# Forgetting attention: the per-head sums of squares of q and k in four reduced-precision passes over a high and a low half

## The reference, cut to what matters

```python
def fox_mixer(h, w_in, b_f, q_gain, k_gain, w_out):
    proj = h @ w_in
    q, k, v, g, f_logit = jnp.split(proj, [...], axis=-1)
    log_f = jax.nn.log_sigmoid(f_logit + b_f)
    qh = rms_norm(to_heads(q, FOX_HEADS), q_gain)   # y = x * rsqrt(mean(x*x over the 64 of a head) + EPS) * gain
    kh = rms_norm(to_heads(k, FOX_HEADS), k_gain)
    vh = to_heads(v, FOX_HEADS)
    o = fox_attention(qh, kh, vh, cumsum of log_f)  # causal softmax(q.k/8 + c[t] - c[s]) @ v
    return (o * jax.nn.silu(g)) @ w_out
```

## Time and profile before

| | |
|---|---|
| three runs, median | 1498.22 us |
| profiled execution, own time | 1497.39 us |
| its span (first to last instruction) | 1495.6 us |
| PE busy | 95% of the span |
| DVE busy | 64% |
| ACT busy | 47% |
| chain that ended last | PE 76%, DVE 13%, ACT 8% |

### The profile page before, as it was taken

One profiled execution on the slowest core, in us unless ns is written; L12 is line 12 of the kernel. 1 busy time (PEld: TensorE's weight loads), 2 busy tenths in 40 slices (PEclk: granted clock), 3 DMA queues, 4 the chain that ended last, 5 costly groups with the idle time before them and its releaser, 6 DMA issues.

```text
span 1495.6 us, 18290 instructions
## 1 busy us (share of the span) xinstructions
PE 1414.9 (95%) x7056; PEld 1190.4 (80%) x7056; DVE 955.8 (64%) x1333; ACT 703.5 (47%) x932; POOL 75.6 (5%) x82
## 2 busy tenths in 40 slices
PE   4899999999999999999979999999999999996996
PEld 3788887888888888888868889787878888885875
DVE  6898886444554444444469776546888778886474
ACT  4677767332342223222246444435456666565251
POOL 3000000000110000000020000020100000000211
PEclk9999999999999999999988999999999999997997
DMA  5111011322222232222311211322312111111211
GB/s 196 57 57 57 1 57 57 113 85 89 108 85 102 96 112 85 97 99 85 110 63 54 84 56 60 124 85 85 116 56 82 56 56 56 56 60 67 85 57 56
DMA packets 19242, 118.22 MB, mean 79 GB/s; under 512 B 2401, under 2 KB 3681, under 8 KB 5617
## 3 DMA queue, kind: packets, MB, share of 16 engines
q1 hardware_dynamic: 18896, 116.38, 21.8%
q0 software_dynamic: 288, 1.05, 0.2%
HBM read 115.32 MB, written 2.10 MB: 79 GB/s over the span
## 4 chain that ended last, share of the span: by engine, by line
PE 76%; DVE 13%; ACT 8%; issue 2%; DMA 0%; DVEq 0%; ACTq 0%
PE ps L508 23%; PE ps L510 23%; PE ps L509 23%; DVE wlo L1637 2%; PE ps L975 1%; PE ps L698 1%; PE ps L944 1%; DVE att L1894 1%; DVE acc L384 1%; ACT att L1217 1%; PE ps L579 1%; DVE atlo L1898 1%; PE ps L962 1%; ACT att L1215 1%; ACT att L1213 1%
## 5 line engine op out<-in xcount | busy, mean ns | idle before, releaser
L508 PE MATMUL ps<-uhi,whi 128*128 128x512 f32 x1104 | 442.5, 401 | 8.4 <-DVE ulo L1698 3.0
L510 PE MATMUL ps<-uhi,wlo 128*128 128x512 f32 x1104 | 433.1, 392 | 0.0
L509 PE MATMUL ps<-ulo,whi 128*128 128x512 f32 x1104 | 432.9, 392 | 0.0
L1637 DVE TENSOR_TENSOR wlo<-wraw,whi 128x2048 fp32r<-128x2048 f32 x105 | 243.5, 2321 | 103.1 <-ACT whi L1088 101.6
L1088 ACT ACTIVATE whi<-wraw 128x2048 fp32r<-128x2048 f32 x105 | 200.3, 1908 | 178.8 <-PE ps L510 178.4
L508 PEld LDWEIGHTS ps<-uhi,whi 128*128 128x128 f32 x1104 | 209.3, 190 | 56.6 <-issue 9.6
L510 PEld LDWEIGHTS ps<-uhi,wlo 128*128 128x128 f32 x1104 | 209.3, 190 | 45.4
L509 PEld LDWEIGHTS ps<-ulo,whi 128*128 128x128 f32 x1104 | 209.6, 190 | 43.6 <-issue 1.9
L508 PE MATMUL ps<-hdhi,whi 128*128 128x512 f32 x256 | 99.6, 389 | 0.0
L509 PE MATMUL ps<-hdlo,whi 128*128 128x512 f32 x256 | 99.6, 389 | 0.0
L510 PE MATMUL ps<-hdhi,wlo 128*128 128x512 f32 x256 | 99.6, 389 | 0.0
(11 more groups left out here) (405 smaller groups left out, 2484.1 us busy)
## 6 DMA issues: line engine op xcount, KB each, us to landing
wraw<-wstream SPq DMA_DIRECT2D x105, 1024.0 KB, 4.8
h<-xT SPq DMA_DIRECT2D x4, 512.0 KB, 5.7
outT<-pp SPq DMA_DIRECT2D x8, 256.0 KB, 2.2
s5b<-s5p_d SPq DMA_DIRECT2D x1, 1024.0 KB, 12.0
pe_in<-pT POOLq DMA_DIRECT2D x2, 512.0 KB, 3.8
cst_in<-cst_d SPq DMA_DIRECT2D x5, 64.0 KB, 10.1
reset<-cst_d SPq DMA_DIRECT2D x1, 256.0 KB, 11.1
ones<-cst_d SPq DMA_DIRECT2D x1, 64.0 KB, 2.1
```

Of the source, the lines that this page charges most:

```text
L508: nc.tensor.matmul(out, lh, rh, start=start, stop=False, skip_group_check=True)
L509: nc.tensor.matmul(out, lh, rl_, start=False, stop=False, skip_group_check=True)
L510: mm = nc.tensor.matmul(out, ll, rh, start=False, stop=stop, skip_group_check=True)
L1637: V.tensor_tensor(wlo[:, slot, :], wraw[:, slot, :], whi[:, slot, :], ALU.subtract).then_inc(lo_done, 1)
```

## The change

ACT's square now writes its result in F32R (`sqhi`). DVE squares `qk` too, in F32 and into `f_y`, and subtracts `sqhi` to get the low half `sqlo` (F32R; it shares its place in memory with `f_half`). PE multiplies both halves with an F32R copy of the block matrix, `headonesr`, so that there are four F32R matmuls for the two F32 ones, and waits for DVE's low half (`sq_lo`) and no longer for ACT's square. In the loop the new DVE pair stands between the evacuation of k and `probs_lo(1)`; for pair 0 it stands behind `fox_prepare`, and so behind the scan. A semaphore of another block (`sgp`) makes room: `ple_gate` uses `step` in its place.

```diff
             def fox_qk_sums(i):
-                pe.wait_ge(qk_sq, i + 1)
+                pe.wait_ge(sq_lo, i + 1)
                 for k in range(2):
-                    mm = nc.tensor.matmul(ps[:, Z0 + k, :], headones[:, :], qksq[:, k, :], start=True, stop=True)
+                    nc.tensor.matmul(ps[:, Z0 + k, :], headonesr[:, :], sqhi[:, k, :], start=True, stop=False)
+                    mm = nc.tensor.matmul(ps[:, Z0 + k, :], headonesr[:, :], sqlo[:, k, :], start=False, stop=True)
                 mm.then_inc(qk_ss, 1)
...
-                A(qksq[:, :, :], qk[:, :, :], ACT.Square).then_inc(qk_sq, 1)
+                A(sqhi[:, :, :], qk[:, :, :], ACT.Square).then_inc(qk_sq, 1)
...
-                        V.tensor_tensor(sg[:, m % 2, :], sg[:, m % 2, :], pp[:, m, :], ALU.mult).then_inc(sgp, 1)
-                        dve.wait_ge(sgp, 8 * layer + m + 1)
+                        step(V.tensor_tensor(sg[:, m % 2, :], sg[:, m % 2, :], pp[:, m, :], ALU.mult))
...
             def fox_prepare():
                 own.do(V.tensor_scalar(gq8[:, :], vec("fox_q_norm"), 0.125, None, ALU.mult))
+                own.do(V.tensor_copy(headonesr[:, :], headones[:, :]))
...
+            def fox_squares_lo(i):
+                step(V.tensor_tensor(f_y[:, :, :], qk[:, :, :], qk[:, :, :], ALU.mult))
+                dve.wait_ge(qk_sq, i + 1)
+                V.tensor_tensor(sqlo[:, :, :], f_y[:, :, :], sqhi[:, :, :], ALU.subtract).then_inc(sq_lo, 1)
...
                     fox_evac(i + 1, 1)
+                    dve.wait_ge(qk_copy, i * 2 + 4)
+                    fox_squares_lo(i + 1)
...
             fox_prepare()
+            dve.wait_ge(qk_copy, 2)
+            fox_squares_lo(0)
             fox_qk_norm(0)
```

More of the change, by code:

```diff
@@ L268, in build @@
                 qk = sb("qk", [P, 2, T], F32, s)
-                qksq = sb("qksq", [P, 2, T], F32, s)
+                sqhi = sb("sqhi", [P, 2, T], F32R, s)
                 f_t = sb("f_t", [P, 2, T], F32, s)
+                with scope() as z:
+                    sqlo = sb("sqlo", [P, 2, T], F32R, z)
                 f_half = sb("f_half", [P, 2, T], F32, s)
@@ L281, in build @@
                 ptlo = sb("ptlo", [P, NZ], F32R, s)
+                headonesr = sb("headonesr", [P, P], F32R, s)
                 nmax = sb("nmax", [P, TT], F32, s)
@@ L375, in build @@
         pe_hi, pe_ready, pp_done, sg_done = sem("ple_hi"), sem("ple_ready"), sem("ple_proj"), sem("ple_sigmoid")
-        sgp = sem("ple_gated")
+        sq_lo = sem("fox_squares_ready")
         out_ready = sem("out_ready")
@@ L2358, in _ @@
             with nc.vector.Fori(0, FOX_PAIRS - 1) as i:
-                own.enter(i, 16)
+                own.enter(i, 17)
                 fox(i)
```

## The result

The changed kernel takes 1500.24 us (median of 20 runs, 1497.9 to 1502.53), the kernel before 1497.93 us in the 20 runs beside it (1494.6 to 1500.9): a ratio of 1.0016, 95% interval 1.0010 to 1.0022, so 2.4 us slower (1.5 to 3.3). The forecast was +2.7 us. A ratio compares all runs of two kernels, so the distances in us given with it can differ from that of the medians. The profiled execution has a span of 1498.3 us, 2.7 more than the one before.

A forecast was written before the change was run, and what follows sets the result against it. PE was taken to bound the loop, and a chain of waits through ACT and DVE the stretch ahead; -3.2 + 5.15 + 0.8 = +2.7 us gave 1500.1 us profiled, 1500.9 median, 8-in-10 range 1498.2 to 1503.0.

The forecast's parts named there:

- The loop: Seven loop bodies: PE's sums shrink by 0.81 us, the new wait leaves 0.46 a body, -3.2 us in all.
- the restart of PE after its pause: Loop sums: the first matmul after a pause takes 0.34 us to the next start, not 0.23.
- what becomes late: Loop, PE's wait for `fvT`: still met, 0.1 us before PE; any larger PE gain would be cut there.
- The head: Ahead of the loop: pair 0's low half stands behind the scan, so sums and logarithm come later, +5.15 us.
- The projection: First projection of the loop: half clock after a 2 us PE pause costs 0 to 1.7 us, taken at +0.8.
- The wait between DVE's square and its subtraction: DVE's subtraction starts 0.13 us after its square in the loop and 0.03 us after it ahead of the loop.
- Edits at nothing: The `headonesr` copy, `sgp` against `step`, and ACT's F32R output were all taken to cost nothing.
- B: Rival: the low half comes later in the loop and the stall eats its gain; +6, 1504.2 us, chance 0.07.
- C: Rival: slack behind pair 0's sums covers the head, leaving the loop's gain; -3.2, 1495.0 us, chance 0.05.
- A: Rival: loop and head as forecast, half clock falls on the projection in full; +3.7, 1501.9 us, chance 0.25.
- D: Rival: no half clock at pair 0's sums or the projection; +1.1, 1499.3 us, chance 0.18.

The follow-up runs named there:

- e1: Changed kernel with the new sums in the seven loop bodies only, pair 0 keeping the old ones: 1493.76 us against 1498.62 for the kernel before, ratio 0.9977.
- e2: Changed kernel with the new sums for pair 0 only, the loop bodies keeping the old ones: 1505.43 us, ratio 1.0048 to the kernel before.
- e4: Changed kernel with both high-half matmuls first, behind ACT's square alone, then both low halves: 1497.13 us, ratio 0.9997 to the kernel before.

## Why the prediction was right, step by step

- **The loop, forecast -0.46 a body, -3.2 in all; measured -0.33, -2.3.** The mechanism was right: DVE's square starts beside ACT's (1165.83 both), the subtraction follows it after 0.13 us, PE wakes 0.05 us behind that, and a quarter of a microsecond is to spare for `fvT` (0.1 was forecast). One term was mis-sized, the restart of PE after its pause, through a slip in reading: the step compared the start of the projection's first matmul, 1163.79, with the chain's 1164.25, and these are two different counts. While PE's queue is full a matmul is recorded 0.17 us ahead of its place in the chain: the sums of the body of the earlier trace rows stand at 1162.53 in the chain and in the timeline of the kernel before at

```profile
1162.36 1.88 PE L944 MATMUL ps<-qksq,headones 128*128 128x512 f32 x4
```

  After a pause there is no such lead, and the chain gives the first matmul its full 0.50. End with end, the step would have read 1162.76 + 0.50 + 3 x 0.23 = 1163.95 against 1164.24, 0.29 us; that end stands in the prediction too, in its paragraph on what becomes late. The restart is 0.27 us (0.50 less 0.23) and not 0.11 (0.34 less 0.23).
- **The head, forecast +5.15; measured +4.98.** The square starts 0.07 us before the scan's end (1096.16 against 1096.23) and not 0.04 behind it, as the two don't depend on each other; the four at half clock take 2.04 us up to the logarithm, 2.07 were forecast.
- **The projection, taken at +0.8 with 0 to 1.7.** In the profiled execution it is 1.54 (7.15 less 5.61). Over 20 runs nothing of it can be seen: loop and head alone give 4.98 - 2.31 = +2.67, measured are +2.4 (1.5 to 3.3), which leaves -0.3, give or take 0.9. So +0.8 is beyond the edge of what the runs allow, and it made up for the 0.9 us by which the loop term was too good.
- **The total is partly luck.** The profiled execution took 1500.10 us, to the hundredth what was forecast for it. But its own terms add up to 4.98 - 2.31 + 1.54 = +4.2, and its span grew by 2.7. The other -1.5 lie outside the stretch that the prediction worked out: the evacuation of pair 0's k comes 0.49 us earlier (1092.36 to 1091.87), and 1.0 us goes between the loop's last scores (1346.99 to 1350.73, +3.7) and the end (+2.7). What brings those two is open.
- **The wait between DVE's square and its subtraction, taken at 0.13 in the loop and 0.03 ahead of it,** measured just that (1167.05 to 1167.18 and 1097.35 to 1097.38). The Trainium skill, VectorE: DVE Perf Modes, section "The DRAIN you can't avoid", says that a semaphore between two DVE operations costs nothing extra. The trace agrees ahead of the loop and not in it, though the two waits are the same. Had it cost nothing in the loop either, a body would have gained 0.43.
- **Edits at nothing:** ACT's square takes 1.06 us with the F32R result as it did before. The copy `headonesr` takes DVE 0.22 us, and the pause ahead of the evacuation of k shrinks from 0.96 to 0.82. In the first `ple_gate` the gap between the two instructions is 0.03 us in both kernels.
- **Rivals.** B (the stall eats the loop's gain) and C (the head is covered) are out by the body times and by `e1` and `e2`. A's condition, half clock on the projection almost in full, held in the profiled execution (1.54 of 1.7), but its time of 1501.9 did not. D (no half clock at either place) needs the sums of pair 0 at full clock, and no kernel that keeps the long pause showed that.

## What to carry to other kernels

One and the same change can be a gain in a loop where PE never waits and a loss once at its entry, where a chain of waits crosses it. So work out the first pass ahead of the loop by itself, and ask where in the other engine's queue the new work stands: there, two instructions moved ahead of a scan were worth 4.3 us. Of several matmuls behind a wait, let those go first whose operand is there. When a saving is larger than the slack of the next wait, find that wait first: in the loop 0.5 of 0.8 us came through until the evacuation of v was moved up too.

## What the runs showed of the hardware

- A pause of PE cost more than it lasted, at full clock: ahead of the sums (512 columns) 0.27 us more, ahead of the transposes of `e4` (128 columns) 0.20 more after only 0.11 us of idle time. In a body of the changed kernel 0.23 us of idle time and 0.27 of restart make 0.50, and the gain was 0.48 short of its 0.81.
- An F32 matmul of 512 columns costs 0.86 us of PE, two records of 0.43, and an F32R one 0.23: at 3.8 to 1, two for one is still a saving of 0.40.
- A second wait on a DVE instruction cost 0.1 us in the hardware loop: there L2209 with two waits starts 0.13 us after L2207's end, L2210 with one 0.03 us after L2209's (1169.11 to 1169.14). Ahead of the loop L2209 with the same two waits starts 0.03 us after (1099.68 to 1099.71). Whether it is the loop itself or the way in which it states what to wait for is open.
- A pause of 2 us was followed by the half clock in one execution and not in another, in kernels whose work is alike up to that point: the scores of the loop's body 0 in the kernel before, and in `e1_loop_only`:

```profile
1107.24 0.49 PE L972 MATMUL ps<-fka,fq 128*128 128x512 f32 x1 [1.99 <-DVE fkb L2237]
1107.57 0.39 PE L974 MATMUL ps<-fkb,fq 128*128 128x512 f32 x1
```
